# Expert items of 96 token slots instead of 128 in a two-layer hybrid encoder trunk

## The reference, cut to what matters

```python
TOKENS = 256; D_MODEL = 1024; D_FF = 3584; N_EXPERTS = 8; TOP_K = 2

def _swiglu(h, w_gate, w_up, w_down):
    return (jax.nn.silu(h @ w_gate) * (h @ w_up)) @ w_down

def _moe(h, router, w_gate, w_up, w_down):
    logits = (hf @ router).astype(jnp.float32)
    top_v, top_i = lax.top_k(logits, TOP_K)
    gates = jax.nn.softmax(top_v, axis=-1)
    dense_gate = jnp.sum(jax.nn.one_hot(top_i, N_EXPERTS) * gates[..., None], axis=1)
    for e in range(N_EXPERTS):
        out = out + dense_gate[:, e:e + 1] * _swiglu(hf, w_gate[e], w_up[e], w_down[e])
```

## Time and profile before

| | |
|---|---|
| time, median of 3 runs | 1992.36 us (1990.65 to 1996.13) |
| span of the profiled execution, first to last instruction | 1997.7 us |
| mean granted TensorE clock over the span | 0.959 |
| PE busy | 1892.7 us, 95% |
| PEld busy | 1509.1 us, 76% |
| DVE busy | 1254.7 us, 63% |
| ACT busy | 999.9 us, 50% |
| read from HBM | 441.09 MB |

### The profile page before, as it was taken

The page is one execution under the profiler, slowest core; times in us unless marked ns, Lnnn a source line. Parts: engine busy times, 40 slices in busy tenths (PEclk is TensorE's granted clock), DMA queues, the critical chain, the costliest instruction groups (busy, mean ns, idle before and its releaser), DMA issues.

```text
span 1997.7 us, 23895 instructions
## 1 busy us (share of the span) xinstructions
PE 1892.7 (95%) x8892; PEld 1509.1 (76%) x8892; DVE 1254.7 (63%) x1298; ACT 999.9 (50%) x1094; POOL 94.3 (5%) x125
## 2 busy tenths in 40 slices
PE   6989987999979989996999999999999999999997
PEld 5868874888868778864787887878878778788785
DVE  1244425444431443426788888878888798888887
ACT  1313124443321423123676766767767677676675
POOL 3012110000000121200000000000000000000000
PEclk9999878999999997986999999999999999999998
DMA  4420004755432410005899999999999999999994
GB/s 167 140 85 1 1 1 142 230 186 176 139 114 72 175 43 1 1 1 179 290 367 318 362 367 307 366 333 341 367 307 367 355 317 367 307 367 367 307 365 169
DMA packets 321404, 442.77 MB, mean 222 GB/s; under 512 B 6804, under 2 KB 271121, under 8 KB 321361
## 3 DMA queue, kind: packets, MB, share of 16 engines
q1 hardware_dynamic: 320196, 438.76, 64.6%
q0 software_dynamic: 1040, 3.38, 0.5%
q10 hardware_dynamic: 124, 0.03, 0.0%
HBM read 441.09 MB, written 1.05 MB: 221 GB/s over the span
## 4 chain that ended last, share of the span: by engine, by line
PE 88%; DVE 6%; ACT 3%; DMA 1%; issue 1%; POOL 0%; SPq 0%; ACTq 0%; DVEq 0%; POOLq 0%
PE bank L1607 13%; PE bank L1609 13%; PE bank L1608 13%; PE bank L1310 7%; PE bank L1631 6%; PE bank L1629 6%; PE bank L1630 6%; PE bank L1573 3%; PE bank L1494 2%; PE bank L1492 2%; PE bank L1704 2%; PE bank L1615 2%; PE bank L1364 1%; PE bank L1741 1%; DMA raw_gu<-in_w_in 1%; PE bank L1481 1%
## 5 line engine op out<-in xcount | busy, mean ns | idle before, releaser
L1098 DVE TENSOR_TENSOR gu_lo<-raw_gu,gu_hi 128x2048 fp32r<-128x2048 f32 x256 | 574.3, 2284 | 9.9 <-ACT gu_hi L824 8.9
L1607 PE MATMUL bank<-gu_hi,xT_hi 128*128 128x512 f32 x1128 | 450.9, 400 | 6.7 <-DVE xT_lo L905 4.5
L1608 PE MATMUL bank<-gu_lo,xT_hi 128*128 128x512 f32 x1128 | 446.8, 396 | 0.0
L824 ACT CAST gu_hi<-raw_gu 128x2048 fp32r<-128x2048 f32 x224 | 416.2, 1908 | 8.5 <-DMA raw_gu<-in_moe_up 8.5
L1103 DVE TENSOR_TENSOR d_lo<-raw_d,d_hi 128x2048 fp32r<-128x2048 f32 x127 | 291.0, 2291 | 132.5 <-ACT d_hi L830 112.5
L1609 PE MATMUL bank<-gu_hi,xg_lo 128*128 128x512 f32 x904 | 358.0, 396 | 0.0
L830 ACT CAST d_hi<-raw_d 128x2048 fp32r<-128x2048 f32 x112 | 213.8, 1909 | 218.4 <-PE bank L1631 218.4
L1607 PEld LDWEIGHTS bank<-gu_hi,xT_hi 128*128 128x128 f32 x1128 | 212.6, 188 | 59.4 <-DVE xT_lo L905 4.9
L1608 PEld LDWEIGHTS bank<-gu_lo,xT_hi 128*128 128x128 f32 x1128 | 212.7, 189 | 52.5 <-issue 1.7
L1629 PE MATMUL bank<-d_hi,hT_hi 128*128 128x512 f32 x560 | 232.4, 415 | 1.7 <-DVE d_lo L1103 1.7
L1631 PE MATMUL bank<-d_hi,hT_lo 128*128 128x512 f32 x560 | 221.7, 396 | 0.0
(11 more groups left out here) (310 smaller groups left out, 2020.0 us busy)
## 6 DMA issues: line engine op xcount, KB each, us to landing
raw_gu<-in_moe_gate SPq DMA_DIRECT2D x114, 1024.0 KB, 6.1
raw_gu<-in_moe_up SPq DMA_DIRECT2D x114, 1024.0 KB, 8.6
raw_d<-in_moe_down SPq DMA_DIRECT2D x113, 1024.0 KB, 7.5
raw_gu<-in_w_in SPq DMA_DIRECT2D x12, 2048.0 KB, 8.1
raw_gu<-in_ff_gate SPq DMA_DIRECT2D x14, 1024.0 KB, 5.1
raw_gu<-in_ff_up SPq DMA_DIRECT2D x14, 1024.0 KB, 7.6
raw_d<-in_ff_down SPq DMA_DIRECT2D x14, 1024.0 KB, 4.9
raw_gu<-in_w_out SPq DMA_DIRECT2D x4, 2048.0 KB, 7.8
```

The source lines that it names most:

```text
L824: nc.scalar.copy(gu_hi[:, v, k], raw_gu[:, v, k]).then_inc(moe.gu_hi, 1)
L1098: TTop(gu_lo[:, slot, k], raw_gu[:, slot, k], gu_hi[:, slot, k].bitcast(F32), ALU.subtract).then_inc(q.gu_lo, 1)
L1607: mm(bank[v][:], hi, gu_hi[:, slot, k], start=k == 0, stop=False)
L1608: mm(bank[v][:], hi, gu_lo[:, slot, k], start=False, stop=False)
```

## The change

An item holds `CAP = 96` token slots. In the expert stage every operand that had the item's 128 tokens on an axis now has 96:

- `gu_products` and `down_products` take 96 stationary columns and write 96 rows; the 512 moving columns stay. ff keeps 128 (`Stream` has a new field `M`, which is P for ff and CAP for moe).
- `gather` keeps `xn` stationary with 128 columns; `sel` moves 96 columns instead of 128, and a group of four results takes 384 columns of its bank instead of 512.
- `transposes` take `h[0:96]` as stationary operand, still 128 columns, and 96 moving columns of the identity.
- The transposes of `selg` (line 1714) get 96 stationary columns and keep 128 moving ones. The scatter contracts over 96 rows; its stationary 128 and moving 512 columns stay.
- ScalarE's and VectorE's passes over these tiles get shorter in the free dimension (`xT_hi`, `xg_lo` 512 to 384, `hT_hi`, `hT_lo` 256 to 192, `sel` 128 to 96) or keep it with 96 partitions (`silu`, `h`, `y_sb`, `selT`).
- An expert may need one item more above 96 tokens and another above 192, so `MAX_ITEMS` is 13, and the routing computes with 16 candidates (8 experts, twice) and 5 further items instead of 8 and 3.

The number of items is still made from the data: 8 plus the number of experts with more than 96 tokens, plus the number of those with more than 192.

```diff
-NE, MAX_ITEMS = 8, 11
+NE, CAP, MAX_ITEMS = 8, 96, 13
+N_ITEMS_AT = 15
...
-        ff, moe = Stream(s, "ff_", 2, 1, 0), Stream(s, "moe_", 1, 0, 1)
+        ff, moe = Stream(s, "ff_", 2, P, 1, 0), Stream(s, "moe_", 1, CAP, 0, 1)
...
-            over, rank, one, val = counts[:, 0], counts[:, 1], counts[:, 2:2 + extra], counts[:, 5:5 + extra]
-            per_item = lambda ap: ap.unsqueeze(1).to_broadcast([P, extra, NE])
-            link(TSop(over, bank[7][:, 32:32 + NE], float(P), None, ALU.is_gt))
-            link(nc.vector.tensor_tensor_scan(rank, ones[:, 0:NE], over, 0.0, ALU.mult, ALU.add))
+            n2 = 2 * NE
+            over, rank, number, shifted = cands[:, 0], cands[:, 1], cands[:, 2], cands[:, 3]
+            one, val = picks5[:, 0:extra], picks5[:, extra:2 * extra]
+            per_item = lambda ap: ap.unsqueeze(1).to_broadcast([P, extra, n2])
+            for c in range(2):
+                TSop(over[:, c * NE:(c + 1) * NE], bank[7][:, 32:32 + NE], float((c + 1) * CAP), None,
+                     ALU.is_gt)
+                last = nc.vector.tensor_copy(number[:, c * NE:(c + 1) * NE], iota1[:, 0:NE])
+            link(last)
+            link(nc.vector.tensor_tensor_scan(rank, ones[:, 0:n2], over, 0.0, ALU.mult, ALU.add))
...
-            for src, dst in ((pos, item_pos), (picked, item_sel), (dense, item_gate)):
-                for t in range(TT):
-                    last = TTop(eq3[:, 3 * t:3 * t + 3], per_item(src[:, t]), one, ALU.mult)
-                link(last)
-                for t in range(TT):
-                    last = nc.vector.tensor_reduce(dst[:, t, NE:MAX_ITEMS], eq3[:, 3 * t:3 * t + 3], AX.X,
-                                                   ALU.add)
-                link(last)
+            for t in range(TT):
+                for src, dst, shift in ((pos, item_pos, float(CAP)), (picked, item_sel, 0.0),
+                                        (dense, item_gate, 0.0)):
+                    TSop(shifted[:, 0:NE], src[:, t], -shift, None, ALU.add)
+                    link(TSop(shifted[:, NE:n2], src[:, t], -2.0 * shift, None, ALU.add))
+                    link(TTop(val, per_item(shifted), one, ALU.mult))
+                    link(nc.vector.tensor_reduce(dst[:, t, NE:MAX_ITEMS], val, AX.X, ALU.add))
...
-                    hi = xT_hi[:, k, t * P:(t + 1) * P]
-                    lo = xT_lo[:, k, t * P:(t + 1) * P] if q.T == 2 else xg_lo[:, k]
-                    mm(bank[v][:], hi, gu_hi[:, slot, k], start=k == 0, stop=False)
+                    hi = xT_hi[:, k, t * P:t * P + q.M]
+                    lo = xT_lo[:, k, t * P:(t + 1) * P] if q.T == 2 else xg_lo[:, k, 0:q.M]
+                    o = bank[v][0:q.M]
+                    mm(o, hi, gu_hi[:, slot, k], start=k == 0, stop=False)
...
-                    last = nc.tensor.transpose(bank[2 + v][:, c * P:(c + 1) * P], h[:, v, c * P:(c + 1) * P],
-                                               ident[:])
+                    last = nc.tensor.transpose(bank[2 + v][:, c * P:c * P + q.M],
+                                               h[0:q.M, v, c * P:(c + 1) * P], ident[0:q.M, 0:q.M])
...
-                            last = mm(bank[6 + b][:, c * P:(c + 1) * P], xn[:, t, k * P:(k + 1) * P],
-                                      sel[:, t], start=t == 0, stop=t == TT - 1)
+                            last = mm(bank[6 + b][:, c * CAP:(c + 1) * CAP], xn[:, t, k * P:(k + 1) * P],
+                                      sel[:, t, 0:CAP], start=t == 0, stop=t == TT - 1)
```

More of the change, by code:

```diff
@@ L81, with __init__ @@
 class Stream:
-    def __init__(self, s, part, token_tiles, slot0, credit):
-        self.T, self.slot0, self.credit = token_tiles, slot0, credit
+    def __init__(self, s, part, token_tiles, rows, slot0, credit):
+        self.T, self.M, self.slot0, self.credit = token_tiles, rows, slot0, credit
         self.gu_loaded = [s[part + "gu_loaded0"], s[part + "gu_loaded1"]]
@@ L156, in build @@
             ("neg_mask", [P], F32))
-        sel, selg, selT = place(at, ("sel", [TT, P], F32), ("selg", [TT, P], F32),
-                                ("selT", [TT, P], F32))
+        sel, selg, selT, cands, picks5 = place(
+            at, ("sel", [TT, P], F32), ("selg", [TT, P], F32), ("selT", [TT, P], F32),
+            ("cands", [4, 2 * NE], F32), ("picks5", [2 * (MAX_ITEMS - NE), 2 * NE], F32))
         at = top[0]
@@ L857, in _ @@
                 for half in range(2):
-                    nc.scalar.copy(y_sb[:, half * 512:(half + 1) * 512], bank[4 + half][:]
+                    nc.scalar.copy(y_sb[0:CAP, half * 512:(half + 1) * 512], bank[4 + half][0:CAP]
                                    ).then_inc(s["y_evicted"], 1)
@@ L1225, in select @@
                     at_n = bass.ds(n, 1)
-                    TSop(sel[:, t], iota1[:], item_pos[:, t, at_n], item_sel[:, t, at_n], ALU.is_equal,
+                    TSop(sel[:, t, 0:CAP], iota1[:, 0:CAP], item_pos[:, t, at_n], item_sel[:, t, at_n], ALU.is_equal,
                          ALU.mult)
-                    last = TSop(selg[:, t], iota1[:], item_pos[:, t, at_n], item_gate[:, t, at_n],
+                    last = TSop(selg[:, t, 0:CAP], iota1[:, 0:CAP], item_pos[:, t, at_n], item_gate[:, t, at_n],
                                 ALU.is_equal, ALU.mult)
@@ L1604, in gu_products @@
                         pe.wait_ge(q.gu_lo, 2 * tile + 2)
-                    hi = xT_hi[:, k, t * P:(t + 1) * P]
-                    lo = xT_lo[:, k, t * P:(t + 1) * P] if q.T == 2 else xg_lo[:, k]
-                    mm(bank[v][:], hi, gu_hi[:, slot, k], start=k == 0, stop=False)
-                    mm(bank[v][:], hi, gu_lo[:, slot, k], start=False, stop=False)
-                    last = mm(bank[v][:], lo, gu_hi[:, slot, k], start=False, stop=k == KD - 1)
+                    hi = xT_hi[:, k, t * P:t * P + q.M]
+                    lo = xT_lo[:, k, t * P:(t + 1) * P] if q.T == 2 else xg_lo[:, k, 0:q.M]
+                    o = bank[v][0:q.M]
+                    mm(o, hi, gu_hi[:, slot, k], start=k == 0, stop=False)
+                    mm(o, hi, gu_lo[:, slot, k], start=False, stop=False)
+                    last = mm(o, lo, gu_hi[:, slot, k], start=False, stop=k == KD - 1)
                 last.then_inc(q.gu_mm, 1)
@@ L1626, in down_products @@
                     for c in range(2):
-                        o = bank[y0 + half][:]
+                        o = bank[y0 + half][0:q.M]
+                        hi, lo = hT_hi[:, v, c, 0:q.M], hT_lo[:, v, c, 0:q.M]
                         st, fi = first and c == 0, final and c == 1
-                        mm(o, hT_hi[:, v, c], d_hi[:, slot, c, cl], start=st, stop=False)
-                        mm(o, hT_hi[:, v, c], d_lo[:, slot, c, cl], start=False, stop=False)
-                        last = mm(o, hT_lo[:, v, c], d_hi[:, slot, c, cl], start=False, stop=fi)
+                        mm(o, hi, d_hi[:, slot, c, cl], start=st, stop=False)
+                        mm(o, hi, d_lo[:, slot, c, cl], start=False, stop=False)
+                        last = mm(o, lo, d_hi[:, slot, c, cl], start=False, stop=fi)
                 last.then_inc(q.dn_mm, 1)
@@ L1713, in moe_step @@
                     for t in range(TT):
-                        last = nc.tensor.transpose(bank[6][:, t * P:(t + 1) * P], selg[:, t], ident[:])
+                        last = nc.tensor.transpose(bank[6][0:CAP, t * P:(t + 1) * P], selg[:, t, 0:CAP],
+                                                   ident[:])
                     last.then_inc(s["sel_t_mm"], 1)
```

52 lines of the change are left out of this document (28 added, 24 removed).

## The result

The changed kernel takes **1973.06 us** (median of 4 runs, 1969.15 to 1977.84) against 1991.91 for the kernel before on the same chip: a ratio of 0.991, 95% interval 0.988 to 0.993. A later comparison gave 1971.39 (6 runs) against 1990.64 (11 runs), 0.991 [0.989, 0.993]. So it is faster by some 19 us, 0.9%, clear of the spread of the runs. The forecast of 1989.4 was the case with unchanged products; what happened is rival 1, whose end was put at 1968.

The account below looks back on a forecast made before the run. PE was taken to set the pace. Products 0, transposes -6.0, gathers 0, routing +3.0 and number of items 0 gave -3 us, from 1992.4 to 1989.4 us; range 1955 to 1998, the forecast's own 1980 to 1997.5.

Parts of the forecast that it names:

- rival 1: Expert-stage fp32r products: the stationary load is in the 20 ns, so 96 columns run faster; near 1968 us, chance 0.42.
- I take 0, since the nearest rows in shape show no effect: Expert-stage fp32r products: 96 stationary columns leave their time unchanged, 0 us, judged from fp32 projections at several widths.
- In proportion: Expert-stage fp32r products: a quarter of the 20 ns saved on each of 4056, -20 us, result 1969.
- But the DMAs stop that: Expert stage: weight transfers let PE gain only some 3.5 us per item, 28 us in all, not the full 74.
- Transposes, -6.0 us: Expert stage: 224 transposes move 96 columns instead of 128, each 0.027 us shorter, -6.0 us.
- Gathers, 0: Gather: 288 passes stand on the floor of 128 fp32 stationary columns, 0 us; bound -7.7 us.
- Scatter: Expert stage's scatter: 128 stationary and 512 moving columns keep their shape, 0 us.
- Routing, +3.0: Routing before the first gather: more and wider small instructions on the path, +3.0 us, bounds +1 and +5.
- Number of items: Expert stage: at most 84 tokens per expert, below 96, so eight items before and after, 0 us.
- Rivals 2 to 4: Ninth item, 2117 us, chance 0.02; stationary load outlasting products, 2070, 0.06; transposes unchanged, only routing left, 1995.4, 0.08.
- The Trainium skill's two independent ports: PE products: moving and stationary operands are read through separate ports, so the next load costs the running product nothing; supports 0.

Follow-up runs that it names:

- e9: Changed kernel without the expert stage's products with `gu_lo`, all loads and splits kept: 1949.6 us.
- e8: Changed kernel with the 24 small instructions of the routing's last loop made into one product and three reduces: 1980.1 us in one run.
- m5: Network left out; fp32r products alone on PE at several widths, offsets and traffic levels: 233.5 ns per product at 128 stationary and 512 moving columns.
- e7: Changed kernel with 64 bytes put between `gu_lo` and `d_hi`, which moves the down weights: 1976.3 us.
- e11: Changed kernel with batched routing and both weight tiles moved to 192 bytes (modulo 256) from their stationary operands: 1969.33 us, 0.988 of the kernel before.

## Why the prediction was right or wrong, point by point

- **"I take 0, since the nearest rows in shape show no effect."** This is the step that failed. The fp32 rows showed that an fp32 stream hides its loads at every width, and I carried that over to fp32r. It does not carry over: at 2.4 GHz, fp32r products of 512 moving columns pass at anything from 226.7 to 233.5 ns, by the width of the stationary operand and the distance between the two operands. The term taken at 0 measured 6 to 7 ns on 24 of a tile's 36 products, 15.1 us in all, and one or two ns on the other 12. So the forecast of 1989.4 and its own range, 1980 to 1997.5, missed 1973. The prediction had named the term, its price per nanosecond and the fact that the rows did not settle it; the whole range held the result because rival 1 was in it.
- **The bounds and rival 1.** "In proportion" gave 1969, and the result is near it, but the reason given is not what the runs show. Proportion wants a down product as fast as a gate product, 64 columns 5 ns under 96, and 104 columns faster than 112. Measured: 231.5 against 227.1, 230.8 against 227.1, and 233.3 against 231.7. With tiles on multiples of 64 bytes (e3) the same change took 1983.5 in its one run, and an item lost 1.05 us instead of 2.89. So the agreement of rival 1 with 1973 is partly luck, and the term that it had no word for is the place of the operands.
- **"But the DMAs stop that"**, at 3.5 us per item. The bound was too tight: they stop PE at 122.0 us per item (e9), 6.2 under the item before. But they have begun to stop it: in the first item tiles of 8.6 us take the place of 8.41, behind ScalarE's wait for up weights, as rival 1 had it, and that costs 1.1 us there. In items two to eight ScalarE waits up to 1.1 us and PE does not.
- **Transposes, -6.0 us: right.** From the first transpose to the second down product it is 0.41 us (1146.50 to 1146.91 in the trace after) instead of 0.46 (1140.93 to 1141.39), so 0.05 per tile, some 5 us over the stage.
- **Gathers, 0: right.** 32 passes take 3.54 us instead of 3.57 with a quarter fewer moving columns, as the floor by the stationary columns wants. Scatter: unchanged.
- **Routing, +3.0: right**, measured +3.3; and a round of 0.80 was 0.82. e8 shows that it was the small instructions of the loop, since batching them gave 3.0 back.
- **Number of items: right**, 8 items and 9 gathers (the 288 passes of line 1717).
- **Rivals 2 to 4** did not happen: no ninth item, no product over 233.5 ns at any width down to 16, and a load of 96 columns takes 161 ns (163 was read from fp32).
- **The Trainium skill's two independent ports** ("TensorE: Matmul & The Clock Gate", part 2). For fp32r the rows do not fit a stream that takes no notice of its stationary operand: with the moving operand unchanged, the width and the place of the stationary one change the pace by up to 6 ns. Whether a shared port is the cause no run shows. By the spacing of N / 2.4 + 2.5 in the same page of the Trainium skill it would be 109.2 ns at 256 moving columns and 215.8 at 512; m5 has 113.5 and 233.5, and the measurement decides.

What stays open is the mechanism. That the pace depends on the distance modulo 256 bytes, on the width, and on what ran before is shown; that reads of the two operands meet in some part of SBUF is only a reading that would fit. A product without any load beside it was not tried, and neither was a distance other than multiples of 32 bytes. Why a group of products keeps one of two paces, and what sets it in e7, is not explained.

## What to carry to other kernels

When the profile has a residue that follows neither the clock nor a listed operation (here 20 ns of 233), measure it by itself before you price a change by rows of another data type: one kernel of bare products gave some 70 settings in one run, and another reproduced four large kernels to the nanosecond. It does not replace the run in place: at a distance of 32 bytes, and in e7 and e11, the kernel did not keep the pace of the bare products. A change that moves tiles in memory, if only by a table of 160 bytes, can change the pace of products it does not touch, so compare against a version in which only the layout is changed. And shorten a small control part on the critical path by batching it: twenty-four small instructions of 0.16 to 0.24 us that wait for each other cost 3.0 us more than four wide ones.

## What the runs showed of the hardware that was not expected

- fp32r products at 2.4 GHz took 6.8, 13.2 and 20.2 ns beyond the column time at 256, 384 and 512 moving columns (113.5, 173.2 and 233.5 ns), with 128 stationary columns and PE alone.
- With fewer stationary columns this excess shrinks by up to a third, by the operands' distance modulo 256 bytes; 96 columns at 192 bytes take 228.5 ns, at 64 bytes 233.4. It is not monotonic in the width. At 192 bytes, 88 and 96 gain most, 104 and 120 nothing, 16 and 64 little.
- Two paces exist at the same addresses (227.1 and 233.1 at a distance of 32 bytes), and a kernel can stay in one of them for a whole item (e7: 125.2 and 126.5 us by turns).
- m5 saw no effect of DMA, ScalarE or VectorE traffic on the pace: 847 products in 184 us alone, beside 343 GB/s, and beside 251 GB/s with the splits.
